# Scaling of the mixer heads moved from VectorE to ScalarE, with unread TensorE products in its waits

## What is computed

```python
mod = jax.nn.silu(c) @ w_ada + b_ada
sh1, sc1, g1, sh2, sc2, g2 = (m[:, None, :] for m in jnp.split(mod, 6, axis=-1))
h = _rms_norm(x, norm_pre_mix) * (1.0 + sc1) + sh1
# mixer: proj = h @ w_in; 4 retention heads (ro) and 4 GLA heads (go), 128 columns each
ro = _head_layer_norm(ro, ret_norm_w, ret_norm_b)   # (x - mu) * rsqrt(var + EPS) * w + b
ro = jax.nn.silu(rg) * ro
go = _rms_norm(go, gla_norm_w)                      # x * rsqrt(mean(x*x) + EPS) * g
go = jax.nn.silu(gg) * go
out = jnp.concatenate([ro, go], axis=-1) @ w_out
x = x + g1 * _rms_norm(out, norm_post_mix)
h = _rms_norm(x, norm_pre_ffn) * (1.0 + sc2) + sh2
f = shared_expert(h) + routed_experts(h)            # 64 experts, 8 per token
x = x + g2 * _rms_norm(f, norm_post_ffn)
```

## Time and profile before

| what | value |
|---|---|
| median of three runs | 1224.35 us |
| the profiled execution's own time | 1225.67 us |
| its span, first to last instruction | 1223.5 us |
| PE, DVE, ACT, POOL busy | 90%, 74%, 53%, 15% |
| mean granted TensorE clock | 0.950 |
| heaviest entries of the chain that ended last | DMA of in_w_exp_down 28%, PE L1828 11% |

### The profile page before, as it was taken

The page is one execution under the profiler, slowest core; times in us unless marked ns, Lnnn a source line. Parts: engine busy times, 40 slices in busy tenths (PEclk is TensorE's granted clock), DMA queues, the critical chain, the costliest instruction groups (busy, mean ns, idle before and its releaser), DMA issues.

```text
span 1223.5 us, 18540 instructions
## 1 busy us (share of the span) xinstructions
PE 1106.1 (90%) x6014; PEld 811.6 (66%) x6014; DVE 903.4 (74%) x1333; ACT 642.7 (53%) x770; POOL 181.9 (15%) x185
## 2 busy tenths in 40 slices
PE   5999999999989999799999999999999999999700
PEld 3899999865444454467777777777777777777500
DVE  4422443365956777579899999989989888888878
ACT  4332221332421233257787777777777777777501
POOL 1000000000110110112222222222222222221102
PEclk9999999998879999899999999999999999999855
DMA  9542221436974143689999999999999999998996
GB/s 341 188 133 80 80 80 40 157 98 202 315 276 132 44 138 120 235 325 381 380 388 391 391 384 385 387 387 381 373 381 383 373 381 379 375 375 314 352 360 210
DMA packets 86545, 339.34 MB, mean 277 GB/s; under 512 B 12561, under 2 KB 36129, under 8 KB 59122
## 3 DMA queue, kind: packets, MB, share of 16 engines
q1 hardware_dynamic: 70130, 301.16, 67.2%
q0 software_dynamic: 16384, 37.78, 8.8%
HBM read 317.00 MB, written 42.86 MB: 294 GB/s over the span
## 4 chain that ended last, share of the span: by engine, by line
PE 46%; DMA 32%; DVE 14%; ACT 6%; issue 2%; SPq 1%; DVEq 0%; POOL 0%; POOLq 0%; ACTq 0%
DMA arena<-in_w_exp_down 28%; PE ps L1828 11%; DVE down_lo L1648 4%; PE ps L2259 4%; PE ps L2067 4%; ACT down_hi L1120 4%; PE ps L2238 3%; PE ps L2239 3%; PE ps L2240 3%; PE ps L1821 2%; PE ps L2242 1%; PE ps L2105 1%; PE ps L2226 1%; DMA arena<-expert_rows 1%; PE ps L2140 1%
## 5 line engine op out<-in xcount | busy, mean ns | idle before, releaser
L1653 DVE TENSOR_TENSOR gu_lo<-w_gu,gu_hi 128x2048 fp32r<-128x2048 f32 (+1 forms) x128 | 258.7, 2022 | 6.4 <-ACT gu_hi L1114 1.1
L1114 ACT ACTIVATE gu_hi<-w_gu 128x2048 fp32r<-128x2048 f32 (+1 forms) x128 | 217.9, 1703 | 0.0
L1648 DVE TENSOR_TENSOR down_lo<-arena,down_hi 128x2048 fp32r<-128x2048 f32 x64 | 146.7, 2293 | 58.0 <-ACT down_hi L1120 58.0
L2238 PE MATMUL ps<-gu_hi,xT_hi 128*112 128x512 f32 x448 | 182.8, 408 | 3.3 <-DVE xT_lo L1658 2.2
L2239 PE MATMUL ps<-gu_lo,xT_hi 128*112 128x512 f32 x448 | 177.9, 397 | 0.0
L2240 PE MATMUL ps<-gu_hi,xT_lo 128*112 128x512 f32 x448 | 177.3, 396 | 0.0
L1120 ACT ACTIVATE down_hi<-arena 128x2048 fp32r<-128x2048 f32 x64 | 122.7, 1918 | 64.0 <-DMA arena<-in_w_exp_down 56.1
L814 POOL DMA_INDIRECT expert_rows<-arena,row_idx x64 | 69.1, 1079 | 356.2 <-ACT arena L1159 340.1
L2259 PE MATMUL ps<-down_hi,actT_hi 128*112 128x512 f32 x256 | 106.6, 416 | 5.5 <-DVE actT_lo L1643 5.5
L807 POOL DMA_INDIRECT arena<-h_rows,token_idx x64 | 80.6, 1259 | 203.1 <-PE ps L2226 156.1
L1828 PE MATMUL ps<-w_hi,hT_hi 128*128 128x300 f32 x352 | 105.6, 300 | 1.4 <-DVE w_lo L1231 1.4
(11 more groups left out here) (310 smaller groups left out, 1989.8 us busy)
## 6 DMA issues: line engine op xcount, KB each, us to landing
w_gu<-in_w_exp_gate SPq DMA_DIRECT2D x64, 1024.0 KB
w_gu<-in_w_exp_up SPq DMA_DIRECT2D x64, 1024.0 KB
arena<-in_w_exp_down SPq DMA_DIRECT2D x64, 1024.0 KB
arena<-in_w_ada SPq DMA_DIRECT2D x16, 1024.0 KB, 6.9
arena<-in_w_in SPq DMA_DIRECT2D x12, 1200.0 KB, 5.6
arena<-expert_rows SPq DMA_DIRECT2D x9, 1024.0 KB, 13.4
arena<-in_w_ada_first SPq DMA_DIRECT2D x4, 2048.0 KB, 16.2
arena<-expert_rows SPq DMA_DIRECT2D x4, 2048.0 KB, 13.0
```

The costliest lines, as they stand in the source:

```text
L1114: a.activation(gu_hi[b % RING][:, :, ks], w_gu[b % U][:, :, ks], ACT.Copy).then_inc(s_ghi, 1)
L1648: v.tensor_tensor(down_lo[:, :, :], w_dn[b % RING], down_hi[:, :, :].bitcast(F32), ALU.subtract).then_inc(s_dlo, 1)
L1653: v.tensor_tensor(gu_lo[b % U][:, :, ks], w_gu[b % U][:, :, ks], gu_hi[b % RING][:, :, ks].bitcast(F32), ALU.subtract).then_inc(s_glo, 1)
L2238: pe.matmul(out, x_hi, gu_hi[r][:, :, k], start=(k == 0), stop=False)
```

## The change

```diff
+            def heads_scaled(t):
+                a.wait_ge(s_nr, t + 1)
+                for n, at in enumerate((C_RQ, C_GO)):
+                    for h in range(H):
+                        cols = slice(at + h * DV, at + (h + 1) * DV)
+                        o = a.activation(proj[:, t, cols], proj[:, t, cols], ACT.Copy, scale=head_rs[:, t, n * H + h:n * H + h + 1])
+                o.then_inc(s_ng, 1)
...
                 if t == PT:
                     mixed_T(0)
+                    heads_scaled(t - 1)
                 a.wait_ge(s_go, t + 1 if t < PT else PT + H)
                 if t < PT:
                     gla_T(t + 1)
+                    if t:
+                        heads_scaled(t - 1)
...
-                a.activation(proj[0:R, t, C_GG:C_GG + RET_W], proj[0:R, t, C_GG:C_GG + RET_W], ACT.Silu).then_inc(s_ng, 1)
+                o = a.activation(proj[0:R, t, C_GG:C_GG + RET_W], proj[0:R, t, C_GG:C_GG + RET_W], ACT.Silu)
+                if t == PT:
+                    o.then_inc(s_ng, 1)
```

On VectorE, in heads(t), the multiplication by the roots (L1397) stays for the sample tile alone:

```diff
-                    step(v.tensor_tensor(o3, o3, head_rs[0:R, t, n * H:(n + 1) * H].unsqueeze(2).broadcast_to([R, H, DV]), ALU.mult))
+                    if t == PT:
+                        step(v.tensor_tensor(o3, o3, head_rs[0:R, t, n * H:(n + 1) * H].unsqueeze(2).broadcast_to([R, H, DV]), ALU.mult))
```

```diff
+            def idle_products(n, bank, width=FIRST_W):
+
+                for _ in range(n):
+                    pe.matmul(ps[:, bank, 0:width], ident, arena[:, 0:width], start=True, stop=True)
+
+            idle_products(5, 6)
             pe.wait_ge(s_cTs, 1)
...
             for t in range(NT):
                 x_tile_transposed(t)
+                if t < 2:
+                    idle_products((2, 5)[t], 6)
             mod1_product(0)
+            idle_products(1, 6)
             mod1_columns(0)
+            idle_products(8, 6)
             mod1_product(1)
...
                 for half in range(2):
                     if half and 0 < h < H - 1:
                         decay_products(2 * h - 1)
+                    if h == H - 1:
+                        idle_products(2, 5, 512)
                     if 2 * h + half:
                         pe.wait_ge(s_rkve, 2 * h + half)
...
+            idle_products(2, 5, 512)
             pe.wait_ge(s_rste, 1)
             pe.wait_ge(s_roe, H)
```

## The result

The changed kernel takes **1234.46 us** (median of 1231.60, 1233.98, 1234.94 and 1240.54), the kernel before beside it 1225.12 us: ratio **1.009**, 95% interval 1.0058 to 1.0121. A second series, of six runs, gave 1237.69 us and a ratio of 1.0109 [1.0079, 1.0140]. The medians of the two series lie 9.3 and 14.4 us above those of the kernel before beside them (1225.12 and 1223.31), where +4.7 was forecast. The time lies within the range (1221 to 1236), but it is "slower by over 0.5%", which had a chance of 0.33.

The account below looks back on a forecast made before the run. Bounds: TensorE nearly gapless to 290 us, the w_ada load issued behind piece 8 in the GLA loop, TensorE again from 355.79. Sum -0.8 (start) + 2.7 (load 12) + 2.8 (w_out) = +4.7; forecast 1229.0 us, range 1221 to 1236.

Parts of the forecast that it names:

- retention: End of retention: unread products delay the first GLA transposes 3.3 us, full clock returns 4.2; net -0.9 us.
- heads: GLA loop: ScalarE scales 2.5 us per tile, late, behind the outputs; mask of tile 2 +2.7 us, with retention's -0.9.
- w_out: Output projection: late scaling of tile 3 delays the last part of w_out, so TensorE waits +2.8 us.
- start: First tiles: unread products raise TensorE's clock during the transposes, bringing the first modulation product earlier; -0.8 us.
- slower rival: End of retention: the products don't hold full clock into the first GLA tile; +8.9, 1233.3 us; chance 0.22.
- +2.7 for load 12: GLA loop: piece 8 ends 2.7 us later, so load 12 of w_ada is issued 2.7 us later.
- who shifts these shifts all twelve groups: Start: any shift of the chain to the first weights moves all twelve groups of projections alike.
- I keep them and piece 8 at the low clock as before: GLA loop: outputs of tile 2 and piece 8 stay at low clock (0.55, 1.82 us); the following transfers keep 18.8 us.
- lower end: GLA loop: full clock for the outputs and piece 8 would give back 2.4 us, leaving +0.3.
- From 355 us on the shift passes through TensorE, the table and the expert loop unchanged.: After the GLA loop: the summed shift, +4.7 us, reaches the end neither grown nor shrunk.
- Hidden after all: Rival: the delays of w_ada and w_out are absorbed and only the start shows; 1223.6 us; chance 0.12.
- the scaling is ready in time: Faster rival: heads(0) starts where centring ends, load 12 gains 1.45, w_out is in time; -3.2, 1221.2 us; chance 0.14.

Follow-up runs that it names:

- e7: Kernel before plus six unread products in TensorE's wait for w_ada ahead of piece 14 in tile 4; ratio 1.0012, median 1225.19 us.
- a_again: The changed kernel itself, unaltered, measured again; 1237.69 us, ratio 1.0109.
- e1: Changed kernel without any of the unread products, so only the multiplications moved to ScalarE; 1236.36 us, ratio 1.0109.
- e3: Changed kernel with ScalarE's scaling ahead of its wait for the outputs, and for tile 3 ahead of the first mixed tile's copy; 1225.03 us, ratio 1.0018.
- e8: Kernel before with all the change's unread products, heads not moved, plus six more in the wait for w_ada; ratio 1.0020.
- e5: Kernel before with only the unread products of the start; 1222.87 us, ratio 0.9988.
- e2: Kernel before with all the change's unread products, heads not moved; 1225.17 us, ratio 1.0023.
- e10: Changed kernel with the scaling of tiles 0 to 2 only moved ahead of the wait for the outputs; 1231.00 us, ratio 1.0058.
- e11: Changed kernel with early scaling for all tiles, plus six unread products in the wait for w_ada; ratio 1.0021, median 1225.24 us.

## Why the prediction was wrong, and where it was right

The mechanism was right in both places. The terms of retention, heads and w_out were off by at most 1 us each; that of the start came to nothing. What failed is the sum behind them: what half clock costs behind waits that grow was left out. Its signs came out as named but for two: piece 8 is later by 5.4 us and not 2 to 3, and TensorE idles 3.38 us within L2094, a little over its 2 to 3. That the time lies within the range is luck: the range reached so far for the sake of the slower rival, which didn't occur. By the timelines of the profiled executions, before and after:

| step of the prediction | forecast | measured |
|---|---|---|
| start | -0.8 | 0.0 (+0.1 at 72 us) |
| end of retention: products | +3.3 | +3.55 |
| returned by full clock, 290 to 302 us | -4.2 | -4.24 |
| an extra stretch at half clock, 252.6 to 256.0 us | 0 | +1.8 |
| heads on ScalarE, to the outputs of tile 2 | +3.6 | +3.59 |
| outputs of tile 2 and piece 8, all at half clock | 0 | +0.66 |
| pieces 9 to 11 at half clock | 0 | +3.8 |
| last load of w_ada shorter | 0 | -2.1 |
| w_out, to block 2 | +2.8 | +3.8 |
| half clock behind that wait | 0 | +1.8 |
| behind it, to the end of the span (half clock lasts longer from 464.2 us on) | 0 | +2.1 |
| **sum** | **+4.7** | **+14.8** |

Retention and heads together are the forecast's +2.7 for load 12. Of the 10.1 us that the forecast lacks, 0.8 are the start, 1.8 the extra stretch at half clock, 2.4 the outputs and pieces with the shorter load, 1.0 w_out, 1.8 and 2.1 the last two rows. The extra stretch lies where the instructions of both kernels are the same; the profiles of six of the other twelve kernels have one in that place, e7's too, whose edit comes later, so it can't be laid to the change.

The 14.8 us are those of one execution, 6 us above the median of its kernel. Two others, by the same landmarks (us later than before; the forecast with its start):

| landmark | forecast | after | a_again | e1, the move alone |
|---|---|---|---|---|
| outputs of tile 0 | -1.7 | +1.1 | +1.3 | +0.4 |
| outputs of tile 2 | +1.9 | +4.7 | +4.9 | +4.0 |
| first mixed transposes | +1.9 | +7.1 | +7.0 | +4.2 |
| second half of the projection | +4.7 | +12.7 | +10.2 | +9.9 |
| end of the span | +4.7 | +14.8 | +11.9 | +10.4 |

The 3.6 us between the first two rows are the heads, the same in all three. What the clock adds is not: between the outputs of tile 2 and the mixed transposes it is 2.4 and 2.1 us in the changed kernel, and 0.2 in e1, where pieces 9 to 11 ran at full clock.

**Start.** The products raised the clock as forecast: the transposes behind the first five take 1.04 us, not 1.94, and the first modulation product starts at 19.07 us in the timeline, not 20.00. Of these 0.9 us the first projection keeps 0.6. The step that failed is "who shifts these shifts all twelve groups": the third load of w_in takes the gain. The Trainium skill's rule that transposes do not engage the full clock (TensorE: Matmul & The Clock Gate, Part 4) would have given a start worth nothing. It was worth nothing in the end, but the load is the reason; against the rule still stand, and the changed kernel can't test it, since products stand among its transposes.

**Retention.** Right to 0.3 us in both terms (without the extra stretch ahead of it). The slower rival (the clock isn't held) is wrong at the place that it names: the granted clock is 1.00 from 290 to 300 us. That the measured time came near the rival's 1233.3 is a coincidence.

**Heads.** Scaling takes 2.43 us per tile (forecast 2.5), VectorE idles 5.07 us ahead of its first product with the weights (about 5), the outputs of tile 2 shift by 3.59 (3.6), TensorE idles 4.32 ahead of them (4). The Trainium skill's rule against multiplications on ScalarE (ScalarE: Activation LUTs, Rules for kernel authors) points the right way for a reason it doesn't give: the same 2.4 us per tile cost 9 to 11 us of the kernel or nothing that can be measured, by their place (the change against e3).

**The step that failed** is: "I keep them and piece 8 at the low clock as before ... the 5 MB behind it keep their 18.8 us." I ended the half clock with piece 8, because it had ended there before. But TensorE had then idled 0.73 us ahead of the outputs; now it idles 4.32, and the half clock lasts from 320.9 to 341.4 us, 20.5 us instead of 6.8. Pieces 9, 10 and 11 take nearly twice their time, and loads 13 to 15 wait for them. From the end of piece 8 to the end of piece 11 it takes 9.5 us instead of 5.7, and the last transfer of w_ada gave 2.1 back (11.07 us instead of 13.16). So the quoted 18.8 us, from the end of piece 8 to that landing, measured 20.6, and piece 8 itself ended 5.4 us later, not 2.7. In the profile of a_again the half clock ends at 335.1 us, after 13.7 us; pieces 9 to 11 lose only 1.2 us there, but the last transfer of w_ada takes 13.39 us, and the first mixed transposes come at 355.33 all the same. With the outputs, piece 8 and the transfer taken together, the prediction lacked 2.4 us in this place in the one execution and 2.1 in the other. The loop's lower end (+0.3, full clock returned) looked the wrong way: the clock was a cost still to come. A second step failed with it: "From 355 us on the shift passes through TensorE, the table and the expert loop unchanged." From the start of the projection's second half to the end of the span the shift grew by 2.1 us more, by 1.7 in a_again and by 0.5 in e1.

**w_out.** Counted from the mixed transposes, ScalarE's scaling ends 4.9 us behind them (forecast 5.0), heads(3) ends 8.7 behind (8.7), the load is issued 10.5 behind (10.5). Only the landing took 5.66 instead of the 4.9 of the earlier trace rows. The wait was 3.38 (2.8), and 2.50 in a_again. What I did not price: during this wait the clock fell again in the profiled execution, and the two products behind it took 3.39 us. In a_again it did not fall, and they took 1.98.

**The rivals.** *Hidden after all* and *the scaling is ready in time* are wrong for this change; the second describes e3's order, but not its gain: ahead of heads(0) VectorE still waits 1.69 us there, but piece 8 does end earlier, and the kernel is no faster than before, because w_ada takes what load 12 gains: piece 8 ends at 324.21 us instead of 325.80, but piece 14 starts at 342.43 instead of 342.21.

## What to carry to other kernels

Where work is moved to an engine with a program in order, its place in that program matters more than its price: the same 32 instructions cost 9 to 11 us behind a wait they don't need and nothing measurable ahead of it. Where a delay puts TensorE into a wait of some microseconds, ask what half clock behind it would cost, over everything that a transfer waits for; behind the 4.3 us of this case it lasted 10 to 20 us. And a gain is worth what the next late transfer leaves of it: w_in took that of the start, and in e8 w_out stood in the way of what was won in the wait for w_ada.

## What the runs showed of the hardware

The same idle time has more than one outcome. TensorE's clock fell to half behind 0.73 us of waiting ahead of the outputs of tile 2 in the kernel before, in e5 and in e7; it did not fall behind 0.73 and 0.74 us at the same place in e8 and e2, nor behind 0.94 us in e3, e10 and e11. The five in which it held have the unread products at the end of retention, and the three in which it fell don't. One execution each shows this, and the cause is open. Runs of one kernel differ by as much as the parts of the change: 29 runs of the kernel before span 1213.82 to 1229.92 us, with mean granted clocks of 0.946 to 0.957, and the longer runs have, as a rule, the lower clock.

An earlier issue of a load need not be an earlier landing: the third load of w_in was issued 0.68 us earlier and landed at 66.97 us instead of 66.85.
